# Query and key norms of delta heads 0 and 1 computed in the tail of the state space stage

## What is computed

```python
h = rmsnorm(x, norm_mix_w[l]); proj = h @ w_in[l]
...
xbc = jax.nn.silu(causal_dwconv(xbc, conv_w) + conv_b.astype(xbc.dtype))
...
y = y * lax.rsqrt(jnp.mean(y * y, axis=-1, keepdims=True) + EPS)      # per group of 512
...
qkv = jax.nn.silu(causal_dwconv(qkv, conv_w)).astype(jnp.float32)
q, k, v = jnp.split(qkv, [GDN_K_DIM, 2 * GDN_K_DIM], axis=-1)
q = q * lax.rsqrt(jnp.sum(q * q, axis=-1, keepdims=True) + EPS) * (GDN_HEAD_K ** -0.5)
k = k * lax.rsqrt(jnp.sum(k * k, axis=-1, keepdims=True) + EPS)
...
o = gdn_scan(q, k, v, g, beta)     # 8 heads of 128: triangular inverse, then 4 chunk steps here
```

## Time and profile before

| | before |
|---|---|
| median of 3 runs | 3074.77 us (3074.44 to 3079.63) |
| profiled execution | 3075.25 us, span 3073.4 us |
| TensorE / VectorE / ScalarE / GpSimd busy | 97% / 53% / 35% / 46% of the span |
| tail of the state space stage, 179 to 246 us | TensorE 51.27 us busy, VectorE 45.54 us |
| delta stage | from 245.8 to about 730 us |

### The profile page before, as it was taken

How to read it: one execution, slowest core, us unless ns; L and a number is a source line. 1 busy time by engine, 2 the same in 40 slices (tenths; PEclk the granted TensorE clock), 3 DMA queues, 4 the chain that set the end, 5 groups by cost and what they waited for, 6 DMA issues and landing times.

```text
span 3073.4 us, 42513 instructions
## 1 busy us (share of the span) xinstructions
PE 2973.8 (97%) x16912; PEld 2385.3 (78%) x16912; DVE 1615.7 (53%) x3311; ACT 1078.8 (35%) x1786; POOL 1412.6 (46%) x1813
## 2 busy tenths in 40 slices
PE   6998999999999999999999999999999999999999
PEld 5877777787888887767877778888877777788887
DVE  5766567566566416659845453333375773433310
ACT  4443333333322223323324432222354553332221
POOL 4553344344556554314323365555443334655554
PEclk9999999999999999999999999999999999999999
DMA  3211112112344431102112222233322112222332
GB/s 126 84 55 59 56 56 69 56 56 78 122 145 144 130 102 60 36 28 67 39 45 67 75 78 94 96 97 99 108 76 69 51 60 81 88 92 97 100 102 86
DMA packets 72359, 248.02 MB, mean 81 GB/s; under 512 B 8161, under 2 KB 8545, under 8 KB 72033
## 3 DMA queue, kind: packets, MB, share of 16 engines
q1 hardware_dynamic: 72160, 245.30, 24.9%
HBM read 243.18 MB, written 2.10 MB: 80 GB/s over the span
## 4 chain that ended last, share of the span: by engine, by line
PE 85%; DVE 11%; ACT 2%; issue 1%; POOL 1%; DMA 0%; SPq 0%; DVEq 0%; ACTq 0%; POOLq 0%
PE bank L1062 24%; PE bank L1064 23%; PE bank L1063 23%; PE bank L1096 3%; PE bank L1110 3%; PE bank L1541 1%; PE bank L1073 1%; PE bank L1559 1%; PE bank L1550 1%; POOL t L2956 1%; DVE sm L1625 1%; DVE t L2171 1%; DVE sm L1627 1%; DVE t L1772 1%; PE bank L1429 0%
## 5 line engine op out<-in xcount | busy, mean ns | idle before, releaser
L2923 POOL TENSOR_TENSOR R<-W,R 128x256 fp32r<-128x256 f32 x1715 | 1293.8, 786 | 1541.7 <-ACT R L2533 1541.6
L1062 PE MATMUL bank<-u,R 128*128 128x512 f32 (+1 forms) x3440 | 1393.1, 405 | 24.3 <-DVE u L1728 8.3
L1064 PE MATMUL bank<-u,R 128*128 128x512 f32 (+1 forms) x3440 | 1349.0, 392 | 0.0
L1063 PE MATMUL bank<-u,R 128*128 128x512 f32 (+1 forms) x3440 | 1348.1, 392 | 0.0
L1062 PEld LDWEIGHTS bank<-u,R 128*128 128x128 f32 (+1 forms) x3440 | 649.2, 189 | 176.9 <-issue 13.5
L1064 PEld LDWEIGHTS bank<-u,R 128*128 128x128 f32 (+1 forms) x3440 | 648.7, 189 | 142.2 <-issue 0.8
L1063 PEld LDWEIGHTS bank<-u,R 128*128 128x128 f32 (+1 forms) x3440 | 650.3, 189 | 128.0 <-issue 5.0
L2533 ACT ACTIVATE R<-W 128x1024 fp32r<-128x1024 f32 (+2 forms) x454 | 452.1, 1001 | 139.0 <-PE bank L1064 132.2
L2563 ACT ACTIVATE u<-t 128x512 fp32r<-128x512 f32 x126 | 78.3, 630 | 313.6 <-DVE t L1750 249.1
L1728 DVE TENSOR_TENSOR u<-t,u 128x512 fp32r<-128x512 f32 x126 | 97.7, 785 | 100.5 <-ACT u L2563 99.8
L1761 DVE SCALAR_TENSOR_TENSOR X<-bank,X 128x512 f32<-128x512 f32 x32 | 22.1, 691 | 237.5 <-PE bank L1064 237.5
(11 more groups left out here) (390 smaller groups left out, 2760.0 us busy)
## 6 DMA issues: line engine op xcount, KB each, us to landing
W<-in_in SPq DMA_DIRECT2D x48, 512.0 KB, 3.3
W<-in_ff_in SPq DMA_DIRECT2D x44, 512.0 KB, 3.3
W<-in_g_qkv SPq DMA_DIRECT2D x24, 512.0 KB, 3.3
W<-in_ada SPq DMA_DIRECT2D x24, 512.0 KB, 3.4
W<-in_f1g SPq DMA_DIRECT2D x22, 512.0 KB, 3.3
W<-in_f1u SPq DMA_DIRECT2D x22, 512.0 KB, 3.2
W<-in_f2g SPq DMA_DIRECT2D x22, 512.0 KB, 3.3
W<-in_f2u SPq DMA_DIRECT2D x22, 512.0 KB, 3.2
```

The costliest lines, as they stand in the source:

```text
L1062: e.matmul(b[0:cols, :], wh, hi, start=(k == 0), stop=False)
L1063: e.matmul(b[0:cols, :], wh, lo, start=False, stop=False)
L1064: i = e.matmul(b[0:cols, :], wl, hi, start=False, stop=(k == KT - 1))
L2923: i = e.tensor_tensor(R[q % NH][:, 1024 + a:1024 + b], W[p % NW][:, a:b], R[q % NH][:, a:b].bitcast(F32), SUB)
```

## The change

The steps `hq`, `hqs`, `hn`, `hnp`, `hn2` of heads 0 and 1 go. In their place are `eq`, `ek`, `ea`, `eb`, `ec`, `ep`, a third chain beside those of the state space stage. They do the same work in bank 5 alone, which is free once the last state is in (`st 1 2`): transposes of q, square to tile 41, transposes of k, square to tile 51, sums, root, scaling, transposes of the scaled k, copy. One bank serves all, so each of the three transposes waits for the reader before, and head 1 for head 0. `hg` of the two heads waits for head 1's k copy, and `hb` now waits for the last normalised tile.

```diff
+EARLY = (0, 1)
+E_Q, E_K = 41, 51
...
+    eq="p.43 s.6", ek="p.43 s.6", ea="v1.6", eb="v3.2", ec="v1.0", ep="p.43 s.6", ...
+    "eq": lambda h: [("conv2", "qkv", 3 * h), ("ep", h - 1) if h else ("st", 1, 2)], "ek": lambda h: [("eq", h), ("conv2", "qkv", 3 * h + 1)],
...
 def gdn_head(h):
-    out = [("hq", h), ("hqs", h), ("hg", h), ("hn", h), ("hnp", h), ("hn2", h), ("hb", h), ("hu", h)]
+    out = ([("hg", h)] if h in EARLY else [("hq", h), ("hqs", h), ("hg", h), ("hn", h), ("hnp", h), ("hn2", h)]) + [("hb", h), ("hu", h)]
...
-    O += weave([chain, normed(0) + normed(1)], convs("xbc", XORD) + convs("qkv", range(6)))
+    early = [(k, h) for h in EARLY for k in ("eq", "ek", "ea", "eb", "ec", "ep")]
+    O += weave([chain, normed(0) + normed(1), early], convs("xbc", XORD) + convs("qkv", range(6)))
...
+            def eq(h):                                  # TensorE
+                w.wait_ge(*(GD.act.at("k", h - 1) if h else SS.dve.at("st", 1, 2)))
+                w.wait_ge(*CV.dve.at("out", "qkv", 3 * h))
+                transpose4(bank[5], t(GS[h].q)).then_inc(*GD.pe.up("qt", h))
+            def ek(h):
+                w.wait_ge(*GD.act.at("sqq", h))
+                w.wait_ge(*CV.dve.at("out", "qkv", 3 * h + 1))
+                transpose4(bank[5], t(GS[h].k)).then_inc(*GD.pe.up("kt", h))
+            def ep(h):
+                w.wait_ge(*GD.dve.at("kt", h))
+                transpose4(bank[5], t(KT_[h])).then_inc(*GD.pe.up("kn", h))
...
             def hg(h):
+                if h in EARLY:
+                    w.wait_ge(*GD.act.at("k", EARLY[-1]))
             def hb(h):
+                if h in EARLY:
+                    w.wait_ge(*SS.dve.at("yn", 7))
...
+            def ea(h):                                  # VectorE
+                w.wait_ge(*GD.act.at("sqk", h))
+                e.tensor_reduce(n[:, 0:4], v3(t(E_K)), AX.X, ADD).then_inc(*GD.dve.up())
+                w.wait_ge(*GD.act.at("sqq", h))
+                e.tensor_reduce(n[:, 4:8], v3(t(E_Q)), AX.X, ADD).then_inc(*GD.dve.up("sums", h))
+                w.wait_ge(*GD.dve.now())
+                e.tensor_scalar(n[:, 0:8], n[:, 0:8], 1e-6, None, ADD).then_inc(*GD.dve.up())
+            def eb(h):
+                newton(GD.dve, n[:, 0:8], n[:, 8:16], n[:, 16:24], n[:, 24:32])
+            def ec(h):
+                e.tensor_tensor(v3(t(KT_[h])), v3(bank[5]), n[:, 16:20].unsqueeze(2).broadcast_to([128, 4, 128]),
+                                MUL).then_inc(*GD.dve.up("kt", h))
+                e.tensor_scalar(n[:, 20:24], n[:, 20:24], 128.0 ** -0.5, None, MUL).then_inc(*GD.dve.up())
+                e.tensor_tensor(n[:, 24:28], n[:, 20:24], n[:, 20:24], MUL).then_inc(*GD.dve.up("ny", h))
...
+            def eq(h):                                  # ScalarE; ek and ep alike
+                w.wait_ge(*GD.pe.at("qt", h))
+                if h:
+                    w.wait_ge(*GD.dve.at("sums", h - 1))
+                e.activation(t(E_Q), bank[5], ACT.Square).then_inc(*GD.act.up("sqq", h))
```

More of the change, by code:

```diff
@@ L295 @@
     pair="s.63 v.75", hq="p.86", hqs="s1.2", hn="v6.9", hnp="p.43", hn2="s.6", hg="p.23 v1.38 s1.23", hb="p.23 v1.5",
-    hu="p1.72 v1.38", i0="g1.3|p.43 s.6 v1.5", il="p.55 s.6", ix="p.43 v.69", iu="p.43 s.6", ip="p.55 v.69", it="p.43 s.6", iq="g1.28", im="p.55 v.69",
+    eq="p.43 s.6", ek="p.43 s.6", ea="v1.6", eb="v3.2", ec="v1.0", ep="p.43 s.6", hu="p1.72 v1.38", i0="g1.3|p.43 s.6 v1.5", il="p.55 s.6", ix="p.43 v.69", iu="p.43 s.6", ip="p.55 v.69", it="p.43 s.6", iq="g1.28", im="p.55 v.69",
     in_="p.55 v.65", hk="p.5 v2.0", hs1="p.22 v.35", hs2="p.22 s.28", hs3="p.54 v.33", ho="s.36", hon="v4.0",
@@ L1605, in tensor @@
             do = dict(dense=dense, nsum=nsum, rmsp=rmsp, scaled=scaled, sums=sums, xd=xd, bt=bt, cb=cb, st=st, ch=ch, sy=sy,
-                      sn1p=sn1p, sn2p=sn2p, i0=i0, il=il, ix=ix, ip=ip, it=it, im=im, in_=in_, iu=iu, hq=hq, hnp=hnp, hg=hg,
+                      sn1p=sn1p, sn2p=sn2p, i0=i0, il=il, ix=ix, ip=ip, it=it, im=im, in_=in_, iu=iu, hq=hq, eq=eq, ek=ek, ep=ep, hnp=hnp, hg=hg,
                       hb=hb, hu=hu, hk=hk, hs1=hs1, hs2=hs2, hs3=hs3, hos=hos, ada2=ada2, ixw=ixw, ixs=ixs, ru=ru, r1p=r1p,
@@ L1952, in in_ @@
                 e.tensor_tensor(t(V_.p), t(V_.p), bank[V_.bx], SUB).then_inc(*IV.dve.up("m", v, n))
+            def ea(h):
+                n = small[GS[h].nw]
+                w.wait_ge(*GD.act.at("sqk", h))
[5 more added lines that the diff above has]
+            def eb(h):
+                n = small[GS[h].nw]
+                newton(GD.dve, n[:, 0:8], n[:, 8:16], n[:, 16:24], n[:, 24:32])
+            def ec(h):
+                n = small[GS[h].nw]
+                w.wait_ge(*GD.dve.now())
+                e.tensor_tensor(v3(t(KT_[h])), v3(bank[5]), n[:, 16:20].unsqueeze(2).broadcast_to([128, 4, 128]),
+                                MUL).then_inc(*GD.dve.up("kt", h))
+                e.tensor_scalar(n[:, 20:24], n[:, 20:24], 128.0 ** -0.5, None, MUL).then_inc(*GD.dve.up())
+                w.wait_ge(*GD.dve.now())
+                e.tensor_tensor(n[:, 24:28], n[:, 20:24], n[:, 20:24], MUL).then_inc(*GD.dve.up("ny", h))
             def hn(h):
@@ L2515, in vector @@
                       conv=conv, conv2=conv2, sums=sums, xd=xd, st0=st0, st=st, ch=ch, cb=cb, cm=cm, sz=sz, sy=sy, sn2=sn2,
-                      sn3=sn3, i0=i0, ix=ix, ip=ip, im=im, in_=in_, hn=hn, hg=hg, hb=hb, hu=hu, hk=hk, hs1=hs1, hs3=hs3,
+                      sn3=sn3, i0=i0, ix=ix, ip=ip, im=im, in_=in_, ea=ea, eb=eb, ec=ec, hn=hn, hg=hg, hb=hb, hu=hu, hk=hk, hs1=hs1, hs3=hs3,
                       hon=hon, ho2=ho2, hz=hz, part=part, branch=branch, ada0=ada0, ada=ada, ada3=ada3, halves=halves,
@@ L2668, in hqs, with ek, ep @@
                 e.activation(t(q.d), bank[q.Z], ACT.Square).then_inc(*GD.act.up("sqq", h))
+            def eq(h):
[3 more added lines that the diff above has]
+                e.activation(t(E_Q), bank[5], ACT.Square).then_inc(*GD.act.up("sqq", h))
+            def ek(h):
+                w.wait_ge(*GD.pe.at("kt", h))
+                e.activation(t(E_K), bank[5], ACT.Square).then_inc(*GD.act.up("sqk", h))
+            def ep(h):
+                w.wait_ge(*GD.pe.at("kn", h))
+                e.activation(t(GS[h].k), bank[5], ACT.Copy).then_inc(*GD.act.up("k", h))
             def hn2(h):
@@ L2906, in scalar @@
             do = dict(split=split, sq=sq, h=h, rb=rb, xg=xg, pair=pair, ffg=ffg, conv=conv, conv2=conv2, sums=sums, bt=bt,
-                      che=che, sz=sz, sn1=sn1, i0=i0, il=il, it=it, iu=iu, hqs=hqs, hn2=hn2, hg=hg, hs2=hs2, ho=ho, hz=hz,
+                      che=che, sz=sz, sn1=sn1, i0=i0, il=il, it=it, iu=iu, eq=eq, ek=ek, ep=ep, hqs=hqs, hn2=hn2, hg=hg, hs2=hs2, ho=ho, hz=hz,
                       gate=gate, ada0=ada0, ixp=ixp, ixs=ixs, sh=sh, wd=wd, ru=ru, r1=r1, r4=r4, rt=rt, s1=s1, ry1a=ry1a,
```

## The result

The changed kernel takes 3083.95 us in the median of 20 executions (3079.11 to 3103.16), the kernel before 3077.22 us in 20 of its own on the same chip (3072.93 to 3080.57). The ratio of the means is 1.0036 (95% interval 1.0025 to 1.0047), that of the medians 1.0022: slower by more than 0.2%. The forecast was no change (3077 us, range 3070 to 3084). The median lies just inside that range, but not by the forecast's reasons, as will be seen.

What follows compares the result with a forecast made beforehand. TensorE, busy 97% of the span, was taken as the bound, losing time where its in-order queue waits on other engines. 11.0 - 3.0 - 0.5 - 2.0 - 3.0 = +2.5 on 3074.77 gave 3077 us, range 3070 to 3084.

Steps and rivals of the forecast that it cites:

- Steps 1 to 4: Tail in four stretches, +11.0 us; third, s_z 6 to last norm's spread, -1.6; fourth, to first g_qkv piece, -0.7.
- step 1: Tail up to s_z 5: VectorE's norm of group 0 delays the state step and y 4; +5.1 us.
- Step 2: Tail from s_z 5 to s_z 6: added sums, root and scaling on VectorE delay y 5; +8.2 us.
- rival B: Slower: TensorE's waits behind VectorE in the tail each drop the clock; sum +8.9, 3083.7 us; chance 0.16.
- case A: Even, the forecast: the tail pays for work moved out of the delta stage; +2.5, between -4.5 and +6; chance 0.62.
- step 7: End of the delta stage: filler pieces cover TensorE's 2.30 us wait and other idle time; -3.0 us (-2 to -3.9).
- Step 6: First pair's output norm: `hos` waits less if one GpSimd split stands earlier; -2.0 us (0 to -3.1).
- step 5: Delta stage: 16 transposes leave TensorE's queue, -3.0 us; a 0.51 us wait for a convolution bank goes, -0.5.

Runs made afterwards that it cites:

- a_st: The changed kernel with the norm of group 0 ordered behind the last state, as in the kernel before: 3087.97 us, +11.5 against the kernel before.
- a_rank: The changed kernel with head 1's transposes no longer counting in the rank of the convolutions they need: 3081.68 us, +4.2 against the kernel before.

## Why the prediction was wrong

**The steps of the tail were right, and their reasons partly not.** Steps 1 to 4 gave +5.1, +8.2, -1.6 and -0.7; measured are +6.3, +8.8, -1.9 and -0.6, in all +12.6 for +11.0 (0.5 of them were there at 176 us already). But step 1 laid its wait to the norm in front of y 4. It stood one instruction earlier, at the last state's matmul, and came from the convolutions that had moved ahead of the states (a_st, a_rank). Step 2 let y 5 wait; y 5 started 6.5 us behind s_z 5 without a wait (214.10), and the root's length fell on the transposes of the scaled k, which stand in TensorE's queue ahead of the sums and s_z 6. Idle time was put at 22 to 26 us and was 20.0; half clock was put at +0.7 and took +5.8. That is the mechanism of rival B, in the tail that case A had forecast: the two errors cancelled, by luck. Moving the waits (a_rank) or the work between them (a_st) gained nothing.

**Steps 5 and 6 were too small, step 7 failed.** From the first g_qkv piece to p_gdn2's first matmul it is 476.6 us before and 467.5 after, -9.1 where -8.5 was forecast. Step 6 had 2.0 for head 0, up to 1.6 of it from the half clock behind the wait. Its wait lost 2.1 us and head 1's 0.6 (0.95 to 0.38), together 2.7; that half clock was a matter of the one execution read, and was worth 0.2 us at most. The larger part is step 5's: in the stage TensorE's busy time fell from 463.1 to 456.7 us, where -3.0 was forecast for the transposes; where the rest comes from stays open. Step 7 (end of the stage, -3.0) is wrong in sign: the idle time from 690 us on was 3.9 and is 4.6 (1.75, 2.68 and 0.17 us), and a half clock of 3.4 us came behind it (1.6). The "five pieces (one of g_z 7, four of p_gdn 6 and 7)" do stand behind head 7's transposes, but the four of p_gdn need VectorE themselves, right where it must make the operands of p_gdn2. What is late next was not asked. So +2.3 for -3.0, and steps 5 and 6 brought some 4 us more than their -5.5; that these cancel is luck too.

**The sum was right for 12 executions of 20.** It was +2.5; those without the long stretch are +3.6 above the kernel before, by errors that cancel and not by the steps as written. Its base was 2 us too low, though: the profiled execution took 3075.25 and the median of three 3074.77, where 20 give 3077.22.

**What failed is the end of the sum.** It has no term behind 730 us, and no reason for leaving it out beyond the equal number of matmuls, panels and DMAs. That part costs nearly the same in the other executions (from p_gdn2's first matmul to the same instruction near 1155 us 429.5 us for 427.8, and the 1.7 are the half clock at 726.9), but in 8 of 20 some 17 us more, by half clock from 1341 us on as far as traces show it, where by time and clock the kernel before has it in 2 of 161. This alone takes the ratio from 1.0012 to 1.0036 and out of the forecast's 0.2%. That the median still lies in the range is luck: its high end was made of case A's upper bound and half of B, and neither holds such a stretch. Rival B put the half clock in the tail, with 1.7 us for a stretch; no case priced a fall behind the stage, where TensorE shows no wait.

**What stays open.** What in the change brings that stretch on. Shown: it comes with any part of the change tried (head 0 alone, without the roots, in another order), on every chip where one of these ran without a delay; a delay of about 1 us at 722 us, of matmuls or of idle time, takes it away (0 of 27, with 3.3 us 1 of 11; for 11 of the 27 the changed kernel without a delay did not run on the same chip). In the 20 traces it goes with where the recurrence lies against the steps of the clock. Not shown: why the kernel before so rarely comes to lie there, why the delay keeps the changed one from it, and why no delay of the kernel before, 1.1 to 5.6 us of matmuls and 6 us of idle time, brings it (1 of 65). Neither the time from the start of the program nor what stands ahead of the recurrence is enough by itself. In the traces the engines' work from 730 to 1330 us is the same.

## What to carry to other kernels

Waits of a matrix engine that runs at its full clock can cost more than their length: here each us of added wait in the tail came with 0.5 to 1.5 us of half clock (five kernels, one trace of each), so the clock's share belongs in the sum at about the size of the wait. A stretch of half clock that one trace shows need not be in the next of the same kernel: look at several before you count it as gained. When filler is moved to cover a wait, look at what the filler itself asks of the engine that is waited for. And where a rank or a planner orders the work, a new chain raises the rank of what it needs: its inputs move too, here three convolutions ahead of the states, which no line of the diff shows.
